# Loads and splits at the borders between stages, and the sums of the modulation with two columns of ones

## The reference

```python
# stack 1, each of 2 layers
a = rms_norm(h, attn_norm[i]); proj = a @ w_in[i]            # three mixers share proj
mix = concat(diff_attention(..), ssd_mixer(..), gla_mixer(..))
h = h + mix @ w_out[i]
f = rms_norm(h, ffn_norm[i])
h = h + (silu(f @ w_ffn_gate[i]) * (f @ w_ffn_up[i])) @ w_ffn_down[i]
h = h + sigmoid(h @ ple_w_gate[i]) * (p[i] @ ple_w_proj[i])   # "PLE"
# stack 2, each of 4 layers (sb, moba, swa, sb)
sh1, sc1, g1, sh2, sc2, g2 = split(silu(c) @ ada_w[i] + ada_b[i], 6)
x = x + g1 * attention_i(rms_norm(x, gain[i, 0]) * (1 + sc1) + sh1)
x = x + g2 * swiglu(rms_norm(x, gain[i, 1]) * (1 + sc2) + sh2)
```

## Time and profile before

| | |
|---|---|
| Median of 3 runs | 2336.46 us (2334.03 to 2341.03) |
| The profiled execution's own time | 2342.8 us |
| Its span, first to last instruction | 2341.0 us |
| Mean granted clock of PE | 0.979 |
| Busy: PE, weight loads of PE, DVE, ACT | 93%, 89%, 68%, 47% |
| HBM | 186 GB/s over the span, some 300 GB/s in the FFNs 0 to 3 |

### The profile page before, as it was taken

The page is one execution under the profiler, slowest core; times in us unless marked ns, Lnnn a source line. Parts: engine busy times, 40 slices in busy tenths (PEclk is TensorE's granted clock), DMA queues, the critical chain, the costliest instruction groups (busy, mean ns, idle before and its releaser), DMA issues.

```text
span 2341.0 us, 44967 instructions
## 1 busy us (share of the span) xinstructions
PE 2185.9 (93%) x17588; PEld 2075.4 (89%) x17588; DVE 1598.4 (68%) x2655; ACT 1092.3 (47%) x1752; POOL 0.2 (0%) x4
## 2 busy tenths in 40 slices
PE   5889999998899999898999999999988999998998
PEld 4779899987798999898999888999887999897998
DVE  4676587756756877566778766778777854666554
ACT  3545444445454443455444455544465444555443
POOL 0000000000000000000000000000000000000000
PEclk8999999999999999999999999999999999999999
DMA  4464399934653998444599544699543965542664
GB/s 125 107 162 147 104 303 300 292 100 110 166 158 104 302 299 282 117 143 138 189 301 297 184 145 131 215 300 298 169 127 122 291 193 166 144 134 83 191 185 135
DMA packets 545379, 436.40 MB, mean 186 GB/s; under 512 B 27472, under 2 KB 470904, under 8 KB 545144
## 3 DMA queue, kind: packets, MB, share of 16 engines
q1 hardware_dynamic: 541904, 431.21, 60.5%
q10 hardware_dynamic: 3368, 3.71, 0.5%
HBM read 433.82 MB, written 1.05 MB: 186 GB/s over the span
## 4 chain that ended last, share of the span: by engine, by line
PE 80%; DVE 9%; ACT 5%; DMA 2%; DVEq 2%; issue 1%; SPq 1%; ACTq 1%
PE bank L644 12%; PE bank L646 12%; PE bank L645 12%; PE acc L644 7%; PE acc L646 7%; PE acc L645 7%; PE bank L788 3%; PE bank L1160 2%; PE bank L844 2%; ACT w_hi L1284 2%; DVE w_lo L1734 1%; PE bank L654 1%; PE bank L709 1%; PE bank L710 1%; PE bank L713 1%
## 5 line engine op out<-in xcount | busy, mean ns | idle before, releaser
L1284 ACT ACTIVATE w_hi<-wslot 128x1024 fp32r<-128x1024 f32 x590 | 610.5, 1054 | 534.2 <-PE acc L646 253.5
L644 PE MATMUL bank<-h_hi,w_hi 128*128 128x256 f32 x2784 | 792.5, 285 | 27.3 <-DVE w_lo L1734 10.6
L645 PE MATMUL bank<-h_lo,w_hi 128*128 128x256 f32 x2784 | 778.3, 280 | 0.0
L646 PE MATMUL bank<-h_hi,w_lo 128*128 128x256 f32 x2784 | 778.3, 280 | 0.0
L1734 DVE TENSOR_TENSOR w_lo<-wslot,w_hi 128x1024 fp32r<-128x1024 f32 x412 | 494.2, 1221 | 219.4 <-ACT w_hi L1284 218.8
L644 PEld LDWEIGHTS bank<-h_hi,w_hi 128*128 128x128 f32 x2784 | 525.7, 189 | 45.4 <-DVE w_lo L1728 14.1
L645 PEld LDWEIGHTS bank<-h_lo,w_hi 128*128 128x128 f32 x2784 | 529.1, 190 | 2.2 <-issue 1.7
L646 PEld LDWEIGHTS bank<-h_hi,w_lo 128*128 128x128 f32 x2784 | 526.5, 189 | 0.0
L644 PE MATMUL acc<-mid_hi,w_hi 128*128 128x256 f32 x1120 | 317.7, 284 | 7.8 <-DVE mid_lo L2279 4.6
L646 PE MATMUL acc<-mid_hi,w_lo 128*128 128x256 f32 x1120 | 312.6, 279 | 0.0
L645 PE MATMUL acc<-mid_lo,w_hi 128*128 128x256 f32 x1120 | 312.6, 279 | 0.0
(11 more groups left out here) (286 smaller groups left out, 2987.1 us busy)
## 6 DMA issues: line engine op xcount, KB each, us to landing
wslot<-in_ada_w_dram SPq DMA_DIRECT2D x192, 512.0 KB, 5.7
wslot<-in_ffn_w_gate_dram SPq DMA_DIRECT2D x88, 512.0 KB, 4.9
wslot<-in_ffn_w_up_dram SPq DMA_DIRECT2D x88, 512.0 KB, 5.4
wslot<-in_ffn_w_down_dram SPq DMA_DIRECT2D x88, 512.0 KB, 3.7
wslot<-in_w_in_dram SPq DMA_DIRECT2D x72, 512.0 KB, 4.8
wslot<-in_sb_w_in_dram SPq DMA_DIRECT2D x48, 512.0 KB, 4.5
wslot<-in_w_ffn_gate_dram SPq DMA_DIRECT2D x44, 512.0 KB, 4.7
wslot<-in_w_ffn_up_dram SPq DMA_DIRECT2D x44, 512.0 KB, 5.4
```

The lines of the kernel that those rows point to most:

```text
L644: pe.matmul(dst, w_hi[:, w, cols], hi, start=start, stop=False, skip_group_check=True)
L645: pe.matmul(dst, w_hi[:, w, cols], lo, start=False, stop=False, skip_group_check=True)
L646: return pe.matmul(dst, w_lo[:, w, cols], hi, start=False, stop=stop, skip_group_check=True)
L1284: return act.activation(dst, src, ACT.Copy)
```

## The change

For each attention that doesn't stand right behind the setup ("early"):

- SP issues the loads of its first two units early: behind the first step of the FFN ahead of it (stack 2), and behind PLE's own loads as before where PLE is ahead. The third load stays in `norm`. In stack 1 the four first loads of PLE move from ahead of the FFN's last step to behind its first.
- ACT writes the two high parts behind the FFN's last chunk, or inside PLE behind the gates 5 and 6; DVE the two low parts at the same places.
- Behind PLE, the first two pairs of squares are made inside PLE, behind the gates 3 and 5, and the last two ahead of the table load of `norm`.
- In the FFNs 2 and 3 ("late"), units 2 and 3 of the last modulation block leave the FFN's last chunk. DVE does them in `norm` behind the additions, PE sums them behind the sum of squares, and DVE stores them behind the eight tiles. PE waits for that store ahead of its first writing of bank 3 in the attention.
- The four sums of a modulation block stream two columns of ones each, into every second column of the bank, and the store reads every second one.

```diff
@@ -189,7 +189,15 @@
...
             counts.update(w_high=1, **slots(SLOT_MIX + 1, [1]))
-        phase("norm", counts, split=split, **more)
+        prior, kinds = phases[-1][0], [kind for kind, _, _ in phases]
+        early = split == "att" and prior != "setup"
+        late = None
+        if early:
+            was = phases[-1][2] if prior == "ple" else phases[len(kinds) - 1 - kinds[::-1].index("ffn")][2]
+            was.update(att_at=dict(at), att=more["att"], att_layer=more["layer"])
+            if prior != "ple" and ada_blocks(was["ada"]) == ADA_STEPS:
+                late = was["ada"], was["start"]
+        phase("norm", counts, split=split, early=early, late=late, squared=prior == "ple", **more)
 
@@ -216,7 +224,7 @@
...
         start = dict(at)
-        phase("ffn", counts, ada=ada, **more)
+        phase("ffn", counts, ada=ada, start=start, att=None, **more)
         add(gate=None if more["stack"] == 1 else (more["layer"], 5), last=("down_done", 0))
@@ -503,6 +511,14 @@
...
 
+            def first_load(kind, l, n, used):
+                w, _, offs = att_weights(kind, l)
+                need = used.get(f"slot{n}", 0) + 1
+                if kind == "swa" and n:
+                    kv_load(w, n, 0, need)
+                else:
+                    load(n, mix_slot(n), unit(w, KT, offs[n]), need)
+
             def ffn_weights(stack, l):
@@ -524,11 +540,8 @@
...
                     w, _, offs = att_weights(ph["att"], ph["layer"])
-                    for n in range(3):
-                        if ph["att"] == "swa" and n:
-                            kv_load(w, n, 0, u[n] + 1)
-                        else:
-                            load(n, mix_slot(n), unit(w, KT, offs[n]), u[n] + 1)
+                    for n in range(2 if ph["early"] and not ph["squared"] else 0, 3):
+                        first_load(ph["att"], ph["layer"], n, at)
                 elif kind == "att":
@@ -603,6 +616,15 @@
...
                     two_steps([None, 2 * P], [0, P], [base[n] + n % 2 + n // 4 for n in range(6)], *block(0), a_base)
+                    if ph["stack"] == 1:
+                        ple_unit(0, ph["layer"], ph["next"])
+                        ple_unit(1, ph["layer"], ph["next"])
+                        for n in range(2):
+                            used = ph["next"].get(f"slot{SLOT_PROJ + n}", 0)
+                            load(SLOT_PROJ + n, wslot[:, SLOT_PROJ + n, :], a["ple_w_proj"][ph["layer"]][P * n:P * n + P, :], used + 1)
+                    elif ph["att"]:
+                        for n in range(2):
+                            first_load(ph["att"], ph["att_layer"], n, ph["att_at"])
                     for lo, hi in runs([block(i)[0] for i in range(NF // 2 - 1)], 1):
@@ -615,12 +637,6 @@
...
                     i = NF // 2 - 1
-                    if ph["stack"] == 1:
-                        ple_unit(0, ph["layer"], ph["next"])
-                        ple_unit(1, ph["layer"], ph["next"])
-                        for n in range(2):
-                            used = ph["next"].get(f"slot{SLOT_PROJ + n}", 0)
-                            load(SLOT_PROJ + n, wslot[:, SLOT_PROJ + n, :], a["ple_w_proj"][ph["layer"]][P * n:P * n + P, :], used + 1)
                     two_steps([(NF - 1) * P, None], [(NF - 2) * P, (NF - 1) * P],
@@ -651,7 +667,7 @@
...
                 for m in range(ADA_SLOTS):
-                    mm = pe.matmul(B(3, m, m + 1), ada_rows[:, P * m:P * m + P], C("ones", 0, 1), start=True, stop=True)
+                    mm = pe.matmul(B(3, 2 * m, 2 * m + 2), ada_rows[:, P * m:P * m + P], C("ones", 0, 2), start=True, stop=True)
                 mm.then_inc(sem["ada_sums"], 1)
@@ -839,6 +855,8 @@
...
                         pe.wait_ge(sem["negmax"], g("negmax") + 2 * i)
+                    else:
+                        pe.wait_ge(sem["ada_stored"], g("ada_stored"))
                     for t in range(TT):
@@ -1159,6 +1177,8 @@
...
                     mm.then_inc(sem["sumsq"], 1)
+                    if ph["late"]:
+                        ada_sum(ph["late"][1], ADA_STEPS - 1)
                     clear_acc()
@@ -1230,7 +1250,7 @@
...
                     down(NF - 1, 1, PART_LAST, last=True)
-                    if blocks == ADA_STEPS:
+                    if blocks == ADA_STEPS and ph["stack"] == 1:
                         ada_sum(at, blocks - 1)
@@ -1318,6 +1338,13 @@
...
                 copy(w_hi[:, part, :], wslot[:, n, :]).then_inc(sem["w_high"], 1)
+
+            def first_high(kind, n, at):
+                mix_high(n, n, unit_loads(at, kind, n, 0))
+
+            def square_pair(q, ready):
+                act.wait_ge(sem["x_ready"], ready)
+                act.activation(sqT[:, 2 * q:2 * q + 2, :], xT[:, 2 * q:2 * q + 2, :], ACT.Square).then_inc(sem["squares"], 1)
 
@@ -1618,15 +1645,13 @@
...
                     act.preload_act_table_set(LN_EXP)
-                    if ph["split"] == "att":
-                        for n in range(2):
-                            mix_high(n, n, unit_loads(at, ph["att"], n, 0))
+                    if ph["split"] == "att" and not ph["early"]:
+                        first_high(ph["att"], 0, at)
+                        first_high(ph["att"], 1, at)
                     if ph["split"] == "ffn":
                         high(1, 3, 16 * (g("slot1") + g("extra1") + 1))
-                    for q in range(4):
-                        act.wait_ge(sem["x_ready"], g("x_ready") - 3 + q)
-                        act.activation(sqT[:, 2 * q:2 * q + 2, :], xT[:, 2 * q:2 * q + 2, :], ACT.Square)\
-                           .then_inc(sem["squares"], 1)
+                    for q in range(0 if ph["squared"] else 4):
+                        square_pair(q, g("x_ready") - 3 + q)
                     act.wait_ge(sem["sumsq"], g("sumsq") + 1)
@@ -1682,8 +1707,11 @@
...
                     step(NF - 1, 1, more=False)
-                    for m in range(2 if ph["stack"] == 1 else 0):
-                        ple_high(m, ph["next"])
+                    for n in range(2):
+                        if ph["stack"] == 1:
+                            ple_high(n, ph["next"])
+                        elif ph["att"]:
+                            first_high(ph["att"], n, ph["att_at"])
                 elif kind == "ple":
@@ -1700,6 +1728,12 @@
...
                             ple_high(m + 5, at)
+                        if m in (5, 6):
+                            first_high(ph["att"], m - 5, ph["att_at"])
+                        if m in (3, 5):
+                            square_pair(m // 2 - 1, g("x_ready") + m // 2)
+                    for q in (2, 3):
+                        square_pair(q, g("x_ready") + q + 1)
 
@@ -1727,6 +1761,9 @@
...
                    .then_inc(slot_used[n], 1)
+
+            def first_low(n, at):
+                low_of(n, n, at.get(f"high{n}", 0) + 1)
 
@@ -1942,7 +1979,7 @@
...
                 c = ADA_SLOTS * block + ADA_SLOTS * ADA_STEPS * ada
-                dve.tensor_tensor(mod_flat[:, bass.ds(c, ADA_SLOTS)], B(3, 0, ADA_SLOTS), ada_bias[:, bass.ds(c, ADA_SLOTS)], ALU.add)\
+                dve.tensor_tensor(mod_flat[:, bass.ds(c, ADA_SLOTS)], bank[:, 3, 0:2 * ADA_SLOTS:2], ada_bias[:, bass.ds(c, ADA_SLOTS)], ALU.add)\
                    .then_inc(sem["ada_stored"], 1)
@@ -2178,9 +2215,13 @@
...
                     w = gain_of(gain)
-                    if ph["split"] == "att":
-                        for n in range(2):
-                            low_of(n, n, g(f"high{n}") + 1)
+                    if ph["split"] == "att" and not ph["early"]:
+                        first_low(0, at)
+                        first_low(1, at)
+                    if ph["late"]:
+                        ada, start = ph["late"]
+                        for n in (2, 3):
+                            ada_unit(start, ada, ADA_STEPS - 1, n, True)
                     if ph["split"] == "ffn":
@@ -2202,6 +2243,8 @@
...
                             h_low(k - 2)
+                    if ph["late"]:
+                        ada_store(start, ada, ADA_STEPS - 1)
                     if shifted and ph["split"] == "att":
@@ -2291,13 +2334,17 @@
...
                     for b in range(2):
-                        step(NF - 2 + b, b, NF // 2 - 1, more=b == 0, block=blocks == ADA_STEPS)
-                    for m in range(2 if ph["stack"] == 1 else 0):
-                        low(PLE_SLOTS[m], PLE_PARTS[m], ph["next"]["w_high"] + m + 1)
+                        step(NF - 2 + b, b, NF // 2 - 1, more=b == 0,
+                             block=blocks == ADA_STEPS and (b == 0 or ph["stack"] == 1))
+                    for n in range(2):
+                        if ph["stack"] == 1:
+                            low(PLE_SLOTS[n], PLE_PARTS[n], ph["next"]["w_high"] + n + 1)
+                        elif ph["att"]:
+                            first_low(n, ph["att_at"])
                 elif kind == "modulation":
...
                     n = ph["ada"]
```

(4 more changed lines are left out.)

## The result

The changed kernel is slower: median 2344.77 us (18 runs), the kernel before 2340.14 us beside it; the ratio of the two is 1.0033, 95% interval 1.0017 to 1.0049, so 7.7 us more (4 to 11.5). The forecast was 8.6 us less. One run of each kernel stands far off (2819.26 and 5501.26 us) and is left out of the ratio. The others scatter over 27 us with the change (2333.67 to 2360.62) and over 11.5 before (2331.48 to 2343.00), and their medians alone lie 4.6 us apart; no run shows all that makes the scatter wider.

What follows compares the result with a forecast made beforehand. PE was taken to bound modulation-carrying FFNs, DMA just behind; gains 11.7 + 8.0 + 4.4 + 1.1 = 25.2 less costs 11.1 + 5.5 = 16.6 gave 8.6 us less: 2336.5 - 8.6 = 2327.9 us, range 2317 to 2337.

Steps and rivals of the forecast that it cites:

- Border behind PLE: At the two borders behind PLE, early high parts and squares let scaling start sooner: 11.7 us gained in both.
- rival (c): Inside PLE squares need another table, so its borders give some 3 us in place of 11.7: 2336.6 us; chance 0.05.
- Ends of stack 1's FFNs: At the two FFN ends, PE time lost to the four PLE loads ahead of the last step returns: 8.0 us.
- Start of the FFNs, the price: Loads behind the first step make PE wait for gate units: 11.1 us in stack 1, 5.5 in stack 2.
- the shift: At the FFN starts, delay of the stream by inserted loads: 5.5 us for stack 1's four, 3.2 for stack 2's two.
- the cover: At the FFN starts, time from the gate unit being ready to PE wanting it: 1.0 to 1.8 us.
- rival (a): At the FFN starts, no cover and a fallen clock at all five, costing 30 us: 2341.3 us; chance 0.14.
- The bound of 30: Upper end of the FFN starts' price: no cover at all, plus 1.5 us each for the clock, 30 us.
- Borders into moba and swa: Scaling starts earlier, partly lost to PE's wait for the late units: 2.4 and 2.0 us gained, together 4.4.
- rival (d): Late units hold up PE: moba and swa borders give nothing, starts cost 4 us more: 2336.3 us; chance 0.11.
- Border into the second sb: Two of three loads behind the late last down unit go: 1.1 us gained, bounds 0 and 1.2.
- Two columns: In the modulation's sums, a second column of ones costs 0, bounds -0.5 and +1 us in all.

Runs made afterwards that it cites:

- spread kernel: Changed kernel with the early loads one by one, behind FFN steps 1, 3, 5, 7 (stack 1) or 3, 7 (stack 2): 2318.05 us, ratio 0.9921.
- two timed kernels: Base with stack 1's four loads, or stack 2's two, in a row behind the FFN's first step again: 2324.18 and 2321.97 us.
- loads alone: Kernel before with only the new, early load places: ratio 1.0046 to the kernel before, 10.8 us slower.
- late sums behind the first tiles: Spread kernel with PE summing the late block behind the attention's first tiles, DVE storing it behind the eight shifts: 2309.61 us, ratio 0.9866.
- loads back: Changed kernel with every early load back at its old place: ratio 0.9993 to the kernel before.
- base: The fastest kernel (spread loads, late sums behind the first tiles) timed once more: 2309.26 us, ratio 0.9882 to the kernel before.
- late units back: Changed kernel with the late units undone, units 2 and 3 again in the FFN's last chunk: ratio 1.0018 to the kernel before.
- spread with late back: Spread kernel with the late units undone as well: 2316.16 us, ratio 0.9898 to the kernel before.
- loads mid-FFN: Changed kernel with its block of early loads behind the FFN's step 5 instead of the first: 2330.04 us, ratio 0.9952 to the kernel before.

## Why the prediction was wrong

**Border behind PLE: right.** Forecast 11.7 us for both; the traces have 12.53 less 6.27 twice, 12.5, and putting it back cost 14.6. The squares between the sigmoids brought no table load: rival (c) is out. To the cheap functions that are in every set by the Trainium skill, "ScalarE: Activation LUTs", section "Table sets: the hidden batching unit" (relu, copy, identity, abs), this trace adds the square, at least beside the sigmoid.

**Ends of stack 1's FFNs: right.** Forecast 8.0. Without PE's wait ahead of the sum of squares, FFN 0 and 1 with their PLE are 229.3 and 229.0 us in the kernel before, against 225.0 and 224.2 in the spread kernel: 9.1 us.

**Start of the FFNs, the price: this step failed.** Forecast 16.6 us. The changed kernel's five FFNs are 6.7, 6.9, 4.6, 3.9 and 4.7 us longer than those of the spread kernel, 26.8 in all, and 27.6 by the two timed kernels. Two terms were too small: the pauses, 17.6 us where I had 13.6, and the clock behind them, 8.5 where I had 3.0; together 26.1. First, the shift: 6.2 us in FFN 0 (9.18 less 3.00) where I took 5.5, and 4.4 in FFN 2 (6.99 less 2.55) where I took 3.2; the cover of 1.1 and 1.5 us was right, since 6.2 less 1.1 is near the 4.96 of idleness, and 4.4 less 1.5 near the 2.78. Second, the clock: I let it fall for pauses of 2.9 us and up, from two rows, and so counted it nowhere in stack 2. It fell behind all five, in stack 2 behind pauses of 2.0 to 2.8 us, one of them shorter than the 2.15 us before with the clock kept; the length of a pause alone doesn't decide it. 1.7 us each is 8.5. Of rival (a) the fallen clock at all five came true, the missing cover didn't: its cost of 30 was 3 too much. Its 2341.3 us is the nearest of the five forecasts; it had 0.14. The bound of 30 stood in my own sum; beside a DMA that was 93% busy the value belonged near it.

**Borders into moba and swa: near in the profiled run by the first product, not in general.** Forecast 2.4 and 2.0 us; there 1.9 and 1.6, and of moba's 1.9 only 0.6 is left where ACT takes up the products. My sum had PE's wait for the late units, but let the clock cost nothing behind it, and what the clock does there differs from one border to the next: the four traces with this order and early loads have eight such borders, each with a PE pause of 1.58 or 1.59 us; behind two the clock stayed, behind four it was down for 3.4 us, behind two for 6.8. The borders took 9.7 to 12.1 and 9.6 to 12.5 us, on average 10.7 and 10.9, a gain of 1.1 and 0.2. The early loads alone gave 3.7 and 3.1, and with the late sums behind the first tiles it is 4.7 and 4.1, so it was the sums' place that took away what the rest of the change gave. That is rival (d), a part of it.

**Border into the second sb: wrong by 2.** Forecast 1.1 less; it was 0.9 us more (6.27 to 7.19), and so in every kernel with the new order of splits and early loads. The last down unit did come earlier (ACT waited 0.23 us for it, 1.19 before), but not because fewer loads stood behind it, as I had it. With the loads back all three stand behind it again, and ACT waited 0.24 us:

```profile
1980.77 1.07 ACT L1304 ACTIVATE w_hi<-wslot 128x1024 fp32r<-128x1024 f32 x1 [0.23 <-DMA wslot<-in_ffn_w_down_dram]
```
```profile
1978.81 0.34 SPq L464 DMA_DIRECT2D wslot<-in_ffn_w_down_dram  x1
1979.19 3.21 SPq L464 DMA_DIRECT2D wslot<-in_sb_w_in_dram  x3
```
```profile
1982.53 1.06 ACT L1301 ACTIVATE w_hi<-wslot 128x1024 fp32r<-128x1024 f32 x1 [0.24 <-DMA wslot<-in_ffn_w_down_dram]
```

So no run shows a delay by the loads behind, and the gain of 0 that I drew from the Trainium skill's ring order is what the loads alone gave: a border of 6.28 us, with 0.21 us of waiting for that unit. What set the 1.19 us before stays open. The border grew because DVE's two low parts stand ahead of the additions: PE's sum of squares starts 0.9 us behind the start of the last product in place of 0.1.

**Two columns: right**, 0.

The sum with these sizes: gains 12.5 + 9.1 + 1.3 - 0.9 = 22.0, costs 26.8, so 4.8 us slower by the traces. The timed kernels give another: the base lies 0.0126 (the mean of its two ratios) or 29.4 us under the kernel before; 14.9 and 12.7 back for the loads at the starts, and 8.6 for the place of the late sums (2318.05 less 2309.4), make the changed kernel 6.8 us slower. Measured: 7.7, with 4.0 to 11.5 as its interval.

## What to carry to other kernels

In a stage where PE and the DMA are both full, price an inserted load at its full transfer time or more wherever PE's lead is smaller than the block, count the clock as lost behind every pause of 2 us or more (at the starts every pause from 2.0 us on had half clock behind it and the two of 1.8 us had not; one of 2.15 us elsewhere was the exception), and insert one load at a time where the lead has built up: here the same fourteen loads cost 27 us in blocks at the start, and when spread no more than 0.4 us of pause at those places in that kernel's trace. Work moved to take a wait from one engine must not be put ahead of work that had nobody to wait for; the late sums cost PE's pause, and often its clock, ahead of the clearing, and nothing to be seen behind the first tiles.

## What the runs showed of the hardware

- PE has two paces at full granted clock. In the last FFN ten of the fourteen traces have 531 or 532 products in the 60 us from 2180, four (before, late units back, spread with late back, loads mid-FFN) have 511 or 512, and the FFN is 190.5 to 191.1 against 184.4 to 185.1 us. No edit goes with it, and a pace is kept for the whole of that FFN. In the trace before, the second half of FFN 4 has the slower one too (512 products in 60 us). What sets it stays open. It is 6 us, as much as the effect asked about, and two single traces can't be compared by their ends for that reason.
- One pause, three outcomes for the clock: behind the same 1.58 us of waiting ahead of the late sums the clock stayed, was down for 3.4 us, or was down for 6.8 us.
- Two loads in stack 2 shifted the stream by 4.4 us, although their 1.05 MB take 3.0 us at the 347 to 350 GB/s of two of the stretches above; four in stack 1 shifted it by 6.2, near the 6.0 of that rate. The loads aren't alike. Where the queue has work waiting, a load of 512 KB in the changed kernel's trace lands, in the median, 1.8 us behind the one ahead of it if it is cut by columns (the gate units of FFN and PLE, moba's units) and 1.3 us if it is made of whole rows (down units, PLE's projections). Two of each make 6.2 us, two by columns 3.6; the other 0.8 us in stack 2 stay open.
